# The border of the state space part and attention: last stores in attention's block, first weight and latents split first

## The chip, the cores and the metric

The kernel runs on one core of one Trainium2 chip. The metric is the device time of a run in microseconds (us), lower is better. A core has TensorE (PE, matmuls), VectorE (DVE), ScalarE (ACT), GpSimd (POOL) and SyncE (SP, which in this kernel issues most DMAs). Each has its own instruction stream; they meet through semaphores and, between blocks of the program, at a barrier.

## The reference

One layer of a hybrid diffusion backbone, for 1024 latent tokens and 256 prompt tokens, width 1024, float32. What matters here:

```
h     = rms_norm(x) * (1 + scale) + shift
q_c, kv_c, k_rope, z, xbc, dt_f, dt_b = split(h @ w_in)
ssm   = rms_norm((ssd(xbc, dt_f) + flip(ssd(flip(xbc), dt_b)) + d_skip * x) * silu(z))   # also returns both final states
q     = rms_norm(q_c) @ w_uq          # 4 heads, 128 nope + 64 rope columns
k, v  = [cache_ckv, rms_norm(kv_c)] @ w_ukv
attn  = softmax((q_nope k_nope^T + rope(q_rope) rope(k_rope)^T) * scale) @ v
x     = x + gate * rms_norm(concat(attn, ssm) @ w_out)
x     = x + gate * rms_norm(swiglu(rms_norm(x) * (1 + scale) + shift))
```

Outputs are both token groups, the prompt's normalised latents and rope keys, and the two final states of the state space part.

## The kernel before

**Precision.** A float32 product is made of three matmuls (`split3`, L407): each operand is split into a high part, a copy in the type fp32r that ACT writes, and a low part, raw minus high, that DVE writes. So each operand costs one ACT and one DVE instruction before PE may use it.

**Stages.** `phase_front` is one block: modulation, norm, input projection, and the state space part, chunk by chunk (ten chunks of 128 tokens, c = 0 to 9; NT = 10). `phase_attention` is the next block, `phase_mix_ffn` the last. Blocks are separated by a barrier of all engines, which stands in the trace under L429 (the end of the front's block).

**Chunk loop of the state space part, SP (L642 to L656).** The normalised latents of query (384 rows, three K tiles) and of key and value (256 rows, two K tiles) and the rope keys were written to DRAM scratch before. As each chunk of the state space part is done, its output `zt(c)` (in `chunks_hi`, rows 4 to 7) is stored to DRAM scratch `ssm_mix_scratch` (L656, after ACT's `mix(c)` has counted `mix_ready`), and when that store has landed, the freed columns take the chunk's latents back from scratch (`load_landed`, L417 to L419; the semaphores q_in, kv_in and kr_in count them by block of 512, 512 and 256 tokens). In the last turn, c = 9, SP first waits for `fin_cp` and stores the two final states from `st_in` to the output (L653), then waits for `mix_ready` 10 and stores the last mix. The columns of chunk 9 are loaded at the start of attention's block (L1639, L1640). Weights of head 0 (`wq_raw`, `wk_raw`, `wv_raw`) and the rope table have been loaded earlier (L638, semaphore w_early).

**Start of attention.** The order is written out by hand on every engine:

- ACT: `split(0)`: high parts of query weight (768 columns in each partition), key weight (256), value weight (512). Then the list `landed`, nine entries: query latents by block (3 x 512, 3 x 512, 3 x 256 columns), kv latents by block (2 x 512, 2 x 512, 2 x 256), cache (512), rope keys (1280), cached rope keys (256), each after its load's semaphore. Then the evictions `high` of keys, fold, query and value.
- DVE: the low parts in the same order (`split(0)`, `split_in(0, 3)` for the query latents), then `rotate(0)`, which multiplies the three rope blocks in PSUM by the rope table, then `split_in(3, 9)`, then the low parts of the evicted products.
- PE: `project(0, kind)` for rope columns of the query, keys, fold (adds the rotated halves), query, value. Rope block b waits for b + 1 entries of `in_lo`, key block b for 4, 5, 7; the first product waits for `w_split` 1. A product of 512 columns of tokens is 3 matmuls for each K tile. Five PSUM banks go round (RING): product n waits for the eviction of product n - 5.
- SP: L1639, L1640, clearing of the front's semaphores, and then for h = 1, 2, 3 the weights of head h, after `w_split` h.

After the projections follows the loop over heads and query tiles; ACT splits head 1's weights at query tile 6 of head 0 (L1665).

Of the kernel before, what the change touches and what calls it, by code (L numbers as in the profile page):

```python
# [23 lines left out]
P = 128  # L24
# [10 lines left out]
T = N_LAT + N_PROMPT  # L35
# [386 lines left out]
def phase_front(L):  # L422
# [6 lines left out]
    with ExitStack() as st:  # L429
# [38 lines left out]

        L.rows = in_hi
        L.table = at("rope_table", "hT_lo", 6 * T * 4, [P, T])  # L470
        L.wq_raw = at("wq_raw", "hT_lo", 7 * T * 4, [P, KQ, 256])
# [119 lines left out]
        def _(sp):  # L591
# [50 lines left out]
            for c in range(NT):  # L642
                if c >= 1:
                    sp.wait_ge(mix_stored, 16 * c)
                    load_landed(L, sp, in_hi, c - 1)
                if c - 1 == 5:
                    sp.dma_start(in_hi[:, 3, 0:2 * N_CACHE].rearrange("p (k t) -> p k t", k=2),
                                 L.kv_s.rearrange("a p t -> p a t")[:, :, T:NKEY]).then_inc(L.cache_in, 16)
                    sp.dma_start(in_hi[:, 3, 2 * N_CACHE:3 * N_CACHE], L.kr_s[:, T:NKEY]).then_inc(L.cache_in, 16)
                if c == NT - 1:  # L650
                    sp.wait_ge(fin_cp, 2)
                    for d in range(2):
                        sp.dma_start(L.outs["ssm"][0, 0, d].rearrange("(a h) p n -> (h p) a n", a=4),  # L653
                                     st_in[:, d, :, :]).then_inc(fin_out, 16)
                sp.wait_ge(mix_ready, c + 1)
                sp.dma_start(quads(L.mixS[c]), zt(c)).then_inc(mix_stored, 16)  # L656

# [884 lines left out]
def phase_attention(L):  # L1542
# [3 lines left out]
    with ExitStack() as st:  # L1546
# [22 lines left out]
        part = lambda raw, hi, lo, c, w, sem, n: (raw, hi[:, :, c:c + w], lo[:, :, c:c + w], sem, n)  # L1569
        landed = ([part(rows[:, 4:7, c:c + w], L.qn_hi, L.qn_lo, c, w, L.q_in[b], w // 8) for b, (c, w) in enumerate(BLOCKS)] +  # L1570
                  [part(rows[:, 0:2, c:c + w], L.ckv_hi, L.ckv_lo, c, w, L.kv_in[b], w // 8)
                   for b, (c, w) in enumerate(BLOCKS)] +
                  [part(cache, L.ckv_hi, L.ckv_lo, T, N_CACHE, L.cache_in, 32),
                   (rows[:, 2, :], L.kr_hi[:, 0:T], L.kr_lo[:, 0:T], L.kr_in, 16 * NT),
                   (rows[:, 3, 2 * N_CACHE:3 * N_CACHE], L.kr_hi[:, T:NKEY], L.kr_lo[:, T:NKEY], L.cache_in, 32)])
        rc_ready, rb_ready, in_hi, in_lo = (L.sem("at_" + n) for n in ("rc", "rb", "in_hi", "in_lo"))
# [60 lines left out]
        @block.sync  # L1637
        def _(sp):
            sp.wait_ge(L.mix_stored, 16 * NT)  # L1639
            load_landed(L, sp, rows, NT - 1)  # L1640
            L.clear_old()
            for h in range(1, HEADS):
                sp.wait_ge(w_split, h)
                sp.dma_start(wq_raw[:], L.dram["w_uq"][h]).then_inc(wl, 16)
# [13 lines left out]
        def _(act):  # L1658
            def split(h):
                if h == 0:  # L1660
                    act.wait_ge(L.w_early, 64)
                else:
                    act.wait_ge(wl, 32 * h)
                    act.wait_ge(proj, n_proj(h))
                act.activation(wq_hi[:], wq_raw[:], ACT.Copy).then_inc(w_hi_r, 1)  # L1665
                act.activation(wk_hi[:], wk_raw[:], ACT.Copy).then_inc(w_hi_r, 1)
                if h % 2 == 0:
                    if h >= 2:
                        act.wait_ge(wvl, 16 * (h // 2))
                    act.activation(wv_hi[:], wv_raw[:], ACT.Copy).then_inc(w_hi_r, 1)  # L1670
# [32 lines left out]

            split(0)
            for src, hi, _, sem, n in landed:
# [58 lines left out]
        def _(dve):  # L1764
            c = Chain(dve, dch)

            def split(h):
                dve.wait_ge(w_hi_r, 2 * h + 2 + (h + 1) // 2)
                c.mark(dve.tensor_tensor(wq_lo[:], wq_raw[:], wq_hi[:].bitcast(F32), ALU.subtract))
                c.mark(dve.tensor_tensor(wk_lo[:], wk_raw[:], wk_hi[:].bitcast(F32), ALU.subtract))  # L1770
                if h % 2 == 0:
                    dve.wait_ge(w_hi_r, 2 * h + 3 + h // 2)
                    c.mark(dve.tensor_tensor(wv_lo[:], wv_raw[:], wv_hi[:].bitcast(F32), ALU.subtract))
# [55 lines left out]

            split(0)  # L1830
            split_in(0, 3)
            rotate(0)
            split_in(3, len(landed))
            for kind in order[1:]:
# [53 lines left out]
        def _(pe):  # L1888
            def project(h, kind, only=None):
                for b, n, i in of_kind(h, kind):  # L1890
                    if only not in (None, b):
                        continue
                    if i == 0:
                        pe.wait_ge(w_split, h + 1)
                    if i >= 5:
# [3 lines left out]
                    if h == 0 and kind in ("qrope", "k"):  # L1899
                        pe.wait_ge(in_lo, b + 1 if kind == "qrope" else (4, 5, 7)[b])  # L1900
                    c0, w = stage[kind][b]
# [10 lines left out]
                    else:  # L1912
                        w_hi, w_lo, x_hi, x_lo, kn = ((wk_hi, wk_lo, L.ckv_hi, L.ckv_lo, KKV) if kind == "k" else
                                                      (wq_hi, wq_lo, L.qn_hi, L.qn_lo, KQ))
                        cols = slice(128, 256) if kind == "qrope" else slice(0, 128)
                        for k in range(kn):
                            mm = split3(pe, bank[:, :w], w_hi[:, k, cols], w_lo[:, k, cols], x_hi[:, k, c0:c0 + w],
                                        x_lo[:, k, c0:c0 + w], k == 0, k == kn - 1)
# [1234 lines left out]
```

## Time and profile before

| | |
|---|---|
| median of 3 runs | 1766.49 us (1763.88 to 1767.3) |
| profiled execution | 1768.09 us |
| its span, first to last instruction | 1766.3 us |
| mean granted TensorE clock | 0.982 |
| PE busy | 1677.5 us (95%) |
| DVE busy | 1040.2 us (59%) |
| ACT busy | 725.2 us (41%) |
| first attention matmul | 486.28 us |

The trace holds each instruction with start and duration, what ended an engine's idle time before it, and the clock that PE was granted (1.00 is 2.4 GHz, 0.50 is 1.2 GHz). The border of the change lies at 478 to 502 us of the span. Instructions overlap a little on an engine: the next one starts before the last one's recorded end.

### The profile page before, as it was taken

How to read it: one execution, taken by the hardware profiler on the slowest of the kernel's cores; microseconds unless marked ns; L12 is line 12 of the kernel's file. 1: busy time of each engine (PE TensorE's matmuls, PEld its weight loads, DVE VectorE, ACT ScalarE, POOL GpSimd, SP SyncE). 2: the span in 40 equal slices, each digit the busy share in tenths (PEclk: the TensorE clock that was granted, in tenths of full speed). 3: DMA queues.
4: the chain of work that ended last, by engine and by line, in shares of the span. 5: the costliest groups of instructions: out<-in, count | busy, mean ns of one | idle time of the engine just before them, and what ended most of it. 6: DMA issues, size and time to landing. Idle time of an engine off the chain costs nothing. (4 is left out here: it accounts for less than half of the span.)

```text
span 1766.3 us, 24765 instructions
## 1 busy us (share of the span) xinstructions
PE 1677.5 (95%) x9795; PEld 1500.1 (85%) x9795; DVE 1040.2 (59%) x1581; ACT 725.2 (41%) x1208; POOL 74.6 (4%) x116
## 2 busy tenths in 40 slices
PE   6999899999799999999997999999999998999997
PEld 6787788878678888887887999999999997888885
DVE  5855765328755555574568554555545554467777
ACT  5652323334544444463564333333333333434453
POOL 0100000004300000000000000000000000000000
PEclk9999999999999999999999999999999999999998
DMA  9134242002400000114321222222222225573345
GB/s 370 70 131 139 108 147 75 25 33 54 119 14 19 1 13 1 66 37 156 124 96 37 100 86 84 91 88 93 95 82 85 101 76 194 187 234 97 121 145 196
DMA packets 76290, 176.33 MB, mean 100 GB/s; under 512 B 10352, under 2 KB 26944, under 8 KB 74128
## 3 DMA queue, kind: packets, MB, share of 16 engines
q1 hardware_dynamic: 72080, 169.75, 27.7%
q0 software_dynamic: 4096, 5.01, 0.9%
q8 instruction: 78, 1.28, 0.3%
q14 instruction: 36, 0.29, 0.1%
HBM read 131.02 MB, written 43.70 MB: 99 GB/s over the span
## 5 line engine op out<-in xcount | busy, mean ns | idle before, releaser
L409 PE MATMUL psF<-gv,gu_ring 128*128 128x320 f32 x1232 | 382.5, 310 | 9.2 <-issue 4.6
L410 PE MATMUL psF<-gv,gu_ring 128*128 128x320 f32 x1232 | 382.0, 310 | 0.0
L411 PE MATMUL psF<-gv,gu_ring 128*128 128x320 f32 x1232 | 382.0, 310 | 0.0
L409 PEld LDWEIGHTS psF<-gv,gu_ring 128*128 128x128 f32 x1232 | 232.5, 189 | 10.1 <-issue 9.1
L410 PEld LDWEIGHTS psF<-gv,gu_ring 128*128 128x128 f32 x1232 | 232.4, 189 | 0.0
L411 PEld LDWEIGHTS psF<-gv,gu_ring 128*128 128x128 f32 x1232 | 232.3, 189 | 0.0
L409 PE MATMUL psF<-d_w_ring,d_hid_ring 128*128 128x512 f32 x360 | 141.4, 393 | 6.3 <-DVE d_w_ring L2687 6.3
L410 PE MATMUL psF<-d_w_ring,d_hid_ring 128*128 128x512 f32 x360 | 141.6, 393 | 0.0
L411 PE MATMUL psF<-d_w_ring,d_hid_ring 128*128 128x512 f32 x360 | 141.4, 393 | 0.0
L409 PE MATMUL psP<-hT_hi,win_hi 128*128 128x512 f32 (+1 forms) x336 | 122.9, 366 | 2.3 <-DVE hT_lo L184 1.6
L411 PE MATMUL psP<-hT_hi,win_lo 128*128 128x512 f32 (+1 forms) x336 | 119.7, 356 | 0.0
L410 PE MATMUL psP<-hT_lo,win_hi 128*128 128x512 f32 (+1 forms) x336 | 119.7, 356 | 0.0
L2420 ACT ACTIVATE hraw<-psF 128x320 f32<-128x320 f32 x130 | 56.7, 437 | 152.3 <-PE psF L411 150.8
L2460 ACT ACTIVATE d_hid_ring<-d_hid 128x640 fp32r<-128x640 f32 x72 | 53.3, 740 | 143.2 <-PE psF L411 125.9
L2684 DVE TENSOR_TENSOR d_hid_ring<-d_hid,d_hid_ring 128x640 fp32r<-128x640 f32 x72 | 59.3, 824 | 85.8 <-ACT d_hid_ring L2460 85.5
L409 PEld LDWEIGHTS psF<-d_w_ring,d_hid_ring 128*128 128x128 f32 x360 | 68.5, 190 | 21.6 <-DVE d_hid_ring L2684 7.1
L2633 DVE TENSOR_TENSOR hraw<-hraw,psF 128x320 f32<-128x320 f32 x130 | 62.6, 485 | 41.1 <-ACT hraw L2420 35.0
L1820 DVE TENSOR_TENSOR pt_lo<-psPT,pt_hi 128x512 fp32r<-128x512 f32 (+1 forms) x104 | 58.4, 581 | 40.8 <-ACT pt_hi L1695 40.8
L411 PEld LDWEIGHTS psF<-d_w_ring,d_hid_ring 128*128 128x128 f32 x360 | 68.5, 190 | 14.4
L2416 ACT ACTIVATE gu_ring<-raw_gu 128x512 fp32r<-128x512 f32 x66 | 41.5, 628 | 95.1 <-PE psF L411 95.1
L410 PEld LDWEIGHTS psF<-d_w_ring,d_hid_ring 128*128 128x128 f32 x360 | 68.2, 189 | 14.3
L2616 DVE TENSOR_TENSOR gu_ring<-raw_gu,gu_ring 128x512 fp32r<-128x512 f32 x66 | 45.6, 691 | 49.6 <-ACT gu_ring L2416 49.3
(425 smaller groups left out, 3622.2 us busy)
## 6 DMA issues: line engine op xcount, KB each, us to landing
hid_variants<-hraw SPq DMA_DIRECT2D x77, 320.0 KB, 2.2
d_hid<-hid_variants SPq DMA_DIRECT2D x77, 320.0 KB, 3.0
m_wring<-in_w_mod SPq DMA_DIRECT2D x16, 1024.0 KB, 5.5
d_b<-in_w_down SPq DMA_DIRECT2D x44, 256.0 KB, 3.8
win_raw<-in_w_in SPq DMA_DIRECT2D x18, 512.0 KB, 5.7
w_mod_staged<-in_w_mod SPq DMA_DIRECT2D x16, 512.0 KB, 11.8
raw_gu<-in_w_gate SPq DMA_DIRECT2D x11, 512.0 KB, 3.9
raw_gu<-in_w_up SPq DMA_DIRECT2D x11, 512.0 KB, 4.8
```

The costliest lines, as they stand in the source:

```text
L409: pe.matmul(out, w_hi, x_hi, start=first, stop=False, skip_group_check=onto)
L410: pe.matmul(out, w_hi, x_lo, start=False, stop=False, skip_group_check=onto)
L411: return pe.matmul(out, w_lo, x_hi, start=False, stop=last, skip_group_check=onto)
L1820: dve.tensor_tensor(pt_lo[:, g[0]:g[-1] + 1, r:r + P], psPT[:, (g0 + i) % 2, 0:len(g), :], pt_hi[:, g[0]:g[-1] + 1, r:r + P].bitcast(F32), ...
L2416: act.activation(wv[:, q % R, 0, :], block_of(r, n), ACT.Copy).then_inc(wv_hi, 1)
L2420: act.activation(dst[:, chunk(c)], psA(c), ACT.Copy).then_inc(copied, 1)
L2460: act.activation(ring_h(e, 0), hr[:, e % 3, :], ACT.Copy).then_inc(h_hi, 1)
L2616: dve.tensor_tensor(wv[:, q % R, 1, :], block_of(r, n), wv[:, q % R, 0, :].bitcast(F32), ALU.subtract).then_inc(wv_lo, 1)
L2633: dve.tensor_tensor(dst[:, chunk(c)], src[:, chunk(c)], bank(c), ALU.add).then_inc(added, 1)
L2684: dve.tensor_tensor(ring_h(e, 1), hr[:, e % 3, :], ring_h(e, 0).bitcast(F32), ALU.subtract).then_inc(h_lo, 1)
```

## The change

SP leaves the front's block after the load of chunk 8's latents. The store of the last mix and the two stores of the final states are issued first thing in attention's block, the mix store ahead of the others, and without waits: the barrier orders them. `split(0)` is gone from ACT and DVE; the three weights of head 0 are entries of `landed`, which now has 14: query weight, the three K tiles of the first query block one by one, second query block, key weight, first kv block, third query block, second and third kv block, cache, rope keys, cached rope keys, value weight. DVE makes the first eight before `rotate(0)` (N_ROPE). PE's rope blocks wait for 1, 5 and 8 entries, block 0 besides for its K tile k's entry (k + 2) ahead of that tile's matmuls; key blocks wait for 8, 9 and 11, the value products for all 14. The weights of head 1 are loaded once all 14 are split; `w_split` and `w_hi_r` count from head 1.

```diff
--- before.py
+++ after.py
@@ -467,6 +467,7 @@
 
 
         L.rows = in_hi
+        L.last_mixed, L.st_out = in_hi[:, 4:8, (NT - 1) * P:NT * P], st_in
         L.table = at("rope_table", "hT_lo", 6 * T * 4, [P, T])
         L.wq_raw = at("wq_raw", "hT_lo", 7 * T * 4, [P, KQ, 256])
         L.wk_raw = at("wk_raw", "hT_lo", 7 * T * 4 + KQ * 1024, [P, KKV, P])
@@ -647,13 +648,9 @@
                     sp.dma_start(in_hi[:, 3, 0:2 * N_CACHE].rearrange("p (k t) -> p k t", k=2),
                                  L.kv_s.rearrange("a p t -> p a t")[:, :, T:NKEY]).then_inc(L.cache_in, 16)
                     sp.dma_start(in_hi[:, 3, 2 * N_CACHE:3 * N_CACHE], L.kr_s[:, T:NKEY]).then_inc(L.cache_in, 16)
-                if c == NT - 1:
-                    sp.wait_ge(fin_cp, 2)
-                    for d in range(2):
-                        sp.dma_start(L.outs["ssm"][0, 0, d].rearrange("(a h) p n -> (h p) a n", a=4),
-                                     st_in[:, d, :, :]).then_inc(fin_out, 16)
-                sp.wait_ge(mix_ready, c + 1)
-                sp.dma_start(quads(L.mixS[c]), zt(c)).then_inc(mix_stored, 16)
+                if c < NT - 1:
+                    sp.wait_ge(mix_ready, c + 1)
+                    sp.dma_start(quads(L.mixS[c]), zt(c)).then_inc(mix_stored, 16)
 
         @block.gpsimd
         def _(pool):
@@ -1567,12 +1564,18 @@
         rows = L.rows
         cache = rows[:, 3, 0:2 * N_CACHE].rearrange("p (k t) -> p k t", k=2)
         part = lambda raw, hi, lo, c, w, sem, n: (raw, hi[:, :, c:c + w], lo[:, :, c:c + w], sem, n)
-        landed = ([part(rows[:, 4:7, c:c + w], L.qn_hi, L.qn_lo, c, w, L.q_in[b], w // 8) for b, (c, w) in enumerate(BLOCKS)] +
-                  [part(rows[:, 0:2, c:c + w], L.ckv_hi, L.ckv_lo, c, w, L.kv_in[b], w // 8)
-                   for b, (c, w) in enumerate(BLOCKS)] +
-                  [part(cache, L.ckv_hi, L.ckv_lo, T, N_CACHE, L.cache_in, 32),
+        q0, q1, q2 = (part(rows[:, 4:7, c:c + w], L.qn_hi, L.qn_lo, c, w, L.q_in[b], w // 8)
+                      for b, (c, w) in enumerate(BLOCKS))
+        kv0, kv1, kv2 = (part(rows[:, 0:2, c:c + w], L.ckv_hi, L.ckv_lo, c, w, L.kv_in[b], w // 8)
+                         for b, (c, w) in enumerate(BLOCKS))
+        first_w = [(raw[:], hi[:], lo[:], L.w_early, 64)
+                   for raw, hi, lo in ((wq_raw, wq_hi, wq_lo), (wk_raw, wk_hi, wk_lo), (wv_raw, wv_hi, wv_lo))]
+        landed = ([first_w[0]] + [tuple(x[:, k, :] for x in q0[:3]) + q0[3:] for k in range(KQ)] +
+                  [q1, first_w[1], kv0, q2, kv1, kv2, part(cache, L.ckv_hi, L.ckv_lo, T, N_CACHE, L.cache_in, 32),
                    (rows[:, 2, :], L.kr_hi[:, 0:T], L.kr_lo[:, 0:T], L.kr_in, 16 * NT),
-                   (rows[:, 3, 2 * N_CACHE:3 * N_CACHE], L.kr_hi[:, T:NKEY], L.kr_lo[:, T:NKEY], L.cache_in, 32)])
+                   (rows[:, 3, 2 * N_CACHE:3 * N_CACHE], L.kr_hi[:, T:NKEY], L.kr_lo[:, T:NKEY], L.cache_in, 32),
+                   first_w[2]])
+        N_ROPE, ROPE_AT, K_AT = 8, (1, 5, 8), (8, 9, 11)
         rc_ready, rb_ready, in_hi, in_lo = (L.sem("at_" + n) for n in ("rc", "rb", "in_hi", "in_lo"))
         units = [(h, t) for h in range(HEADS) for t in range(NT)]
         key_tiles = lambda t: list(range(NT_LAT, NT)) if t >= NT_LAT else list(range(NT_LAT)) + [NT, NT + 1]
@@ -1636,11 +1639,18 @@
 
         @block.sync
         def _(sp):
+            sp.dma_start(L.mixS[NT - 1].rearrange("p (a n) -> p a n", n=P), L.last_mixed).then_inc(L.mix_stored, 16)
+            for d in range(2):
+                sp.dma_start(L.outs["ssm"][0, 0, d].rearrange("(a h) p n -> (h p) a n", a=4),
+                             L.st_out[:, d, :, :]).then_inc(L.fin_out, 16)
             sp.wait_ge(L.mix_stored, 16 * NT)
             load_landed(L, sp, rows, NT - 1)
             L.clear_old()
             for h in range(1, HEADS):
-                sp.wait_ge(w_split, h)
+                if h == 1:
+                    sp.wait_ge(in_lo, len(landed))
+                else:
+                    sp.wait_ge(w_split, h - 1)
                 sp.dma_start(wq_raw[:], L.dram["w_uq"][h]).then_inc(wl, 16)
                 sp.dma_start(wk_raw[:], L.dram["w_uk"][h]).then_inc(wl, 16)
                 if h % 2 == 0:
@@ -1657,16 +1667,12 @@
         @block.scalar
         def _(act):
             def split(h):
-                if h == 0:
-                    act.wait_ge(L.w_early, 64)
-                else:
-                    act.wait_ge(wl, 32 * h)
-                    act.wait_ge(proj, n_proj(h))
+                act.wait_ge(wl, 32 * h)
+                act.wait_ge(proj, n_proj(h))
                 act.activation(wq_hi[:], wq_raw[:], ACT.Copy).then_inc(w_hi_r, 1)
                 act.activation(wk_hi[:], wk_raw[:], ACT.Copy).then_inc(w_hi_r, 1)
                 if h % 2 == 0:
-                    if h >= 2:
-                        act.wait_ge(wvl, 16 * (h // 2))
+                    act.wait_ge(wvl, 16 * (h // 2))
                     act.activation(wv_hi[:], wv_raw[:], ACT.Copy).then_inc(w_hi_r, 1)
 
             def high(h, kind):
@@ -1701,7 +1707,6 @@
                     act.wait_ge(o_read, pair)
                 act.activation(rb[:], psO[:, 2 * P:4 * P], ACT.Copy).then_inc(rb_ready, 1)
 
-            split(0)
             for src, hi, _, sem, n in landed:
                 act.wait_ge(sem, n)
                 act.activation(hi, src, ACT.Copy).then_inc(in_hi, 1)
@@ -1765,11 +1770,11 @@
             c = Chain(dve, dch)
 
             def split(h):
-                dve.wait_ge(w_hi_r, 2 * h + 2 + (h + 1) // 2)
+                dve.wait_ge(w_hi_r, 2 * h - 1 + (h + 1) // 2)
                 c.mark(dve.tensor_tensor(wq_lo[:], wq_raw[:], wq_hi[:].bitcast(F32), ALU.subtract))
                 c.mark(dve.tensor_tensor(wk_lo[:], wk_raw[:], wk_hi[:].bitcast(F32), ALU.subtract))
                 if h % 2 == 0:
-                    dve.wait_ge(w_hi_r, 2 * h + 3 + h // 2)
+                    dve.wait_ge(w_hi_r, 2 * h + h // 2)
                     c.mark(dve.tensor_tensor(wv_lo[:], wv_raw[:], wv_hi[:].bitcast(F32), ALU.subtract))
                 c.wait()
                 dve.sem_inc(w_split, 1)
@@ -1827,10 +1832,9 @@
                     dve.wait_ge(in_hi, i + 1)
                     dve.tensor_tensor(lo, src, hi.bitcast(F32), ALU.subtract).then_inc(in_lo, 1)
 
-            split(0)
-            split_in(0, 3)
+            split_in(0, N_ROPE)
             rotate(0)
-            split_in(3, len(landed))
+            split_in(N_ROPE, len(landed))
             for kind in order[1:]:
                 low(0, kind)
             dve.wait_ge(L.fin_out, 32)
@@ -1890,14 +1894,16 @@
                 for b, n, i in of_kind(h, kind):
                     if only not in (None, b):
                         continue
-                    if i == 0:
-                        pe.wait_ge(w_split, h + 1)
+                    if i == 0 and h >= 1:
+                        pe.wait_ge(w_split, h)
                     if i >= 5:
                         pe.wait_ge(drained, n - 4)
                     elif h >= 1:
                         pe.wait_ge(e_ready, h * NT - (0 if i == 4 else 1 if i == 3 else 2))
                     if h == 0 and kind in ("qrope", "k"):
-                        pe.wait_ge(in_lo, b + 1 if kind == "qrope" else (4, 5, 7)[b])
+                        pe.wait_ge(in_lo, (ROPE_AT if kind == "qrope" else K_AT)[b])
+                    elif h == 0 and kind == "v":
+                        pe.wait_ge(in_lo, len(landed))
                     c0, w = stage[kind][b]
                     bank = psS[:, RING[i % 5], :]
                     if kind == "fold":
@@ -1914,6 +1920,8 @@
                                                       (wq_hi, wq_lo, L.qn_hi, L.qn_lo, KQ))
                         cols = slice(128, 256) if kind == "qrope" else slice(0, 128)
                         for k in range(kn):
+                            if (h, kind, b) == (0, "qrope", 0):
+                                pe.wait_ge(in_lo, k + 2)
                             mm = split3(pe, bank[:, :w], w_hi[:, k, cols], w_lo[:, k, cols], x_hi[:, k, c0:c0 + w],
                                         x_lo[:, k, c0:c0 + w], k == 0, k == kn - 1)
                     mm.then_inc(proj, 1)
```

## Rows read from the trace of the kernel before

**Rows 1.** Page, part 1: busy us, share of span, instructions
```profile
PE 1677.5 (95%) x9795; PEld 1500.1 (85%) x9795; DVE 1040.2 (59%) x1581; ACT 725.2 (41%) x1208; POOL 74.6 (4%) x116
```

**Rows 2.** PE's waits over the span: us in total, times, longest us
```profile
PE psScore L409 <- DVE qn_lo L1828: 8.1, 1, 8.1
...
PE psF L409 <- issue: 4.6, 1, 4.6
```

**Rows 3.** Timeline of PE: start, duration, instruction, idle before and releaser
```profile
486.28 0.77 PE L409 MATMUL psScore<-qn_hi,wq_hi 128*128 128x512 f32 x1 [8.12 <-DVE qn_lo L1828]
...
491.31 0.40 PE L409 MATMUL psScore<-qn_hi,wq_hi 128*128 128x512 f32 x1
...
491.54 0.40 PE L410 MATMUL psScore<-qn_lo,wq_hi 128*128 128x512 f32 x1
...
495.56 0.50 PE L409 MATMUL psScore<-ckv_hi,wk_hi 128*128 128x512 f32 x1 [1.65 <-DVE ckv_lo L1828]
...
501.75 0.58 PE L409 MATMUL psScore<-qn_hi,wq_hi 128*128 128x512 f32 x1
```

**Rows 4.** Timeline of SP at the border: start, duration, instruction
```profile
474.78 0.52 SPq L656 DMA_DIRECT2D ssm_mix_scratch<-chunks_hi  x1
477.36 0.37 SPq L417 DMA_DIRECT2D chunks_hi<-q_scratch  x1
...
478.31 0.47 SPq L419 DMA_DIRECT2D chunks_hi<-kr_scratch  x1
...
479.84 0.64 SPq L656 DMA_DIRECT2D ssm_mix_scratch<-chunks_hi  x1
483.31 0.37 SPq L417 DMA_DIRECT2D chunks_hi<-q_scratch  x1
```

**Rows 5.** L429, end of the front's block: drains in ns, start in us
```profile
L429 POOLq DRAIN  x1: 2888/2888/2888, 476.0 to 476.0; - x1
...
L429 ACTq DRAIN  x1: 626/626/626, 478.2 to 478.2; - x1
L429 SPq DRAIN  x1: 368/368/368, 480.5 to 480.5; - x1
```

**Rows 6.** Timeline of ACT: start, duration of all x, idle before
```profile
481.15 0.84 ACT L1665 ACTIVATE wq_hi<-wq_raw 128x768 fp32r<-128x768 f32 x1 [2.35 <-PEq L429]
...
482.20 0.61 ACT L1670 ACTIVATE wv_hi<-wv_raw 128x512 fp32r<-128x512 f32 x1
482.72 2.84 ACT L1707 ACTIVATE qn_hi<-chunks_hi 128x1536 fp32r<-128x1536 f32 x2
485.95 0.84 ACT L1707 ACTIVATE qn_hi<-chunks_hi 128x768 fp32r<-128x768 f32 x1 [0.39 <-DMA chunks_hi<-q_scratch]
486.70 1.99 ACT L1707 ACTIVATE ckv_hi<-chunks_hi 128x1024 fp32r<-128x1024 f32 x2
```

**Rows 7.** Windows: stretch, length, busy of PE, PEld, DVE, ACT, POOL, PEclk, DMA, GB/s
```profile
392.20:398.80 6.60, 6.60 (x18) 4.20 (x19) 0.86 (x1) 2.15 (x2) 2.51 (x3) 0.50 0.03 3
...
490.00:491.00 1.00, 1.00 (x4) 0.81 (x3) 0.51 (x1) 1.00 (x2) 0.00 (x0) 0.50 0.03 8
...
935.00:938.00 3.00, 2.78 (x10) 2.81 (x11) 3.00 (x4) 1.27 (x1) 0.00 (x0) 0.50 0.00 0
```

**Rows 8.** Timeline of DVE
```profile
482.33 0.96 DVE L1769 TENSOR_TENSOR wq_lo<-wq_raw,wq_hi 128x768 fp32r<-128x768 f32 x1 [4.52 <-ACT wk_hi L1666]
...
484.37 4.29 DVE L1828 TENSOR_TENSOR qn_lo<-chunks_hi,qn_hi 128x1536 fp32r<-128x1536 f32 x3
490.49 0.69 DVE L1782 TENSOR_TENSOR q_prod<-psScore,rope_table 128x512 f32<-128x512 f32 x1 [1.83 <-PE psScore L411]
...
494.30 3.55 DVE L1828 TENSOR_TENSOR ckv_lo<-chunks_hi,ckv_hi 128x1024 fp32r<-128x1024 f32 x4
...
499.50 1.88 DVE L1794 TENSOR_TENSOR kn_lo<-psScore,kn_hi 128x512 fp32r<-128x512 f32 x3
```

**Rows 9.** ACT's split of head 1's query weight: ns, first and last start
```profile
L1665 ACT ACTIVATE wq_hi<-wq_raw x1: 833/833/833, 549.0 to 549.0; 128x768 fp32r<-128x768 f32 x1
```

## The prediction

> **What bounds the kernel now.** I read the page first: TensorE (PE) is busy 95% of the span [rows 1], so only time in which it waits or runs at its lower clock can be given back. The list of PE's waits comes next: its longest single wait, 8.1 us, stands before the first matmul of attention, for `qn_lo` [rows 2]. The timeline around it gives the pieces. PE's last work of the state space part ends at 486.28 - 8.12 = 478.16 [rows 3]. Before the barrier between the two blocks (L429) ScalarE (ACT) has drained at 478.2 + 0.63 = 478.83 and GpSimd (POOL) at 476.0 + 2.89 = 478.89, but SyncE (SP) drains only at 480.54 to 480.91, behind its stores [rows 4, 5]. ACT then starts at 481.15 and splits the weights of query, key and value and the first latents before PE may begin [rows 6]. PE runs its first matmuls at half clock (1.2 instead of 2.4 GHz): the stretch 490 to 491 has 0.50 [rows 7], and matmuls of 512 columns then start 0.43 us apart (twice 0.23, the distance between 491.31 and 491.54 [rows 3]). It waits once more, 1.65 us, for `ckv_lo`, and begins the keys at 495.56 and the first query block at 501.75 [rows 3]. VectorE (DVE) has by then been through six splits, 494.30 to 499.50 [rows 8].
>
> **The change, part by part.** I follow the new order to 501.75's counterpart, since from there on the code and the order of work are the old ones.
>
> *Barrier.* SP's last work before it is now the issue of L419, which ends at 478.31 + 0.47 = 478.78; the two state stores (479.84 - 478.78 = 1.06 us with gaps) and the last mix store (0.64) are taken out [rows 4]. From the end of L656 (480.48) to ACT's start (481.15) were 0.67 us [rows 4, 6]. With SP free at 478.78, and POOL's drain over (478.89) before SP's own would be (0.37 from 478.8, so 479.2 [rows 5]), ACT starts at about 479.4: 1.7 us gained. Bounds: 0, if something unseen holds the barrier, and 1.8, where ACT or POOL would end it.
>
> *Stores and last loads.* They are now issued after the barrier, the mix store first: 479.4. Such a store took 474.78 to 477.36 = 2.58 us until the waiting load left, and 3.47 behind the state stores [rows 4]; now it is ahead of them: 2.6, so L417 leaves at 482.0 and, like before (483.31 to 485.95 [rows 4, 6]), is there 2.6 later: 484.6, or 485.5 at the upper bound of both. The state stores have one reader of their end, a wait of DVE (L1836) that stands behind all first projections. The clearing of semaphores behind L417 to L419 has no waiter.
>
> *ACT.* From starts in [rows 6]: 512 columns cost 0.52, 1536 (2.84 - 1.47) = 1.37, so 0.21 for each 256 more; 1024 (1.99 - 1.04) = 0.95; the two weights of 768 and 256 columns 481.15 to 482.20 = 1.05 together, 0.74 and 0.31 by the slope. New order: query weight 479.4 to 480.24 (its own duration 0.84), the three K tiles of the first latents from 480.14, 480.66, 481.18, second latents 481.70 to 483.16, key weight 483.07, first kv block 483.38, and at 484.33 the last latents, which then wait for their load. Even from 485.5 they are done at 486.35.
>
> *DVE.* From [rows 8]: 512 columns cost (1.88 - 0.68)/2 = 0.60, 1536 (4.29 - 0.96)/2 = 1.67; by the slope 0.27 for each 256, 256 cost 0.33, 768 0.87, 1024 1.13. `wq_lo` starts 0.03 behind its high part: 480.27. K tile 0 is split from 481.14 to 481.83. PE began 0.15 after its input before (484.37 + 1.76 = 486.13 to 486.28 [rows 8, 3]): now 481.98 instead of 486.28, 4.30 earlier. The split into three K tiles costs DVE 3 x 0.60 - 1.67 = 0.13, hidden: tiles 1 and 2 are there by 483.03, and PE needs 1.28 us for each at half clock. Then the second latents at 483.2 (ACT), key weight 484.87, kv block 485.20, last latents 486.33, done at 487.29.
>
> *PE.* Rope columns of the query: 18 matmuls at 0.23 and 9 at half that, 5.18 us at full clock, plus half of the slow stretch S. Before, S was 491.0 - 486.28 = 4.7. After another idle time, of 4.6 us [rows 2], the clock was low from 935 to 938 (0.50), with PE busy for most of it [rows 7]; the idle time here is now 3.8. I take S = 3.4, between 2.8 (935 to 938) and 4.7; bounds 0 and 6.6, the last because PE ran 6.6 us on end, wholly busy, at 0.50 in 392.2 to 398.8 [rows 7]. Blocks 0 and 1 end at 481.98 + 4.14 + 1.7 = 487.82, later than the last latents (487.29), so no wait; block 2 ends at 488.86. The keys begin at once, since their first block is split already: 495.56 becomes 488.86, and 1.80 us between the last rope issue (486.28 + 5.18 + 2.35 = 493.8) and 495.56 go.
>
> *What is late next.* DVE now turns the three rope products before it splits the second kv block. The last starts 0.2 after PE's end, 489.05; kv block 1 runs 489.39 to 490.61; PE ends its first key block at 488.86 + 1.38 = 490.24 and waits 0.4. The next input (the cache) is there at 491.8, before 492.0. From there DVE has the old five splits and the value weight: 5.20 - 1.13 + 0.60 = 4.67, so the first `kn_lo` starts at 494.06 and the second ends at 495.35. Before, keys to query block took 501.75 - 495.56 = 6.19 [rows 3]; now 488.86 + 6.19 + 0.4 = 495.45, just not held by `kn_lo`.
>
> *Value weight and next weights.* The value weight moves behind all latents; its 0.60 is in the 4.67. Value products need it 5 us and more after 495. SP loads head 1's weights once everything is split, at about 494.8, some microseconds later than before; they are wanted at 549.0 [rows 9]. That is 50 us of cover; only without it would the delay, under 10 us, count.
>
> *Sum.* 501.75 - 495.45 = 6.3 us: 4.30 (barrier 1.75, order 2.55) + 0.65 (shorter slow stretch) + 1.80 - 0.4, within rounding. It runs on to the end because PE's order behind it is unchanged and relative to its own ends. The profiled execution took 1768.09 (span 1766.3 and 1.8 around it), so it would be 1761.8; the median of the runs shown, 1766.49, is 1.6 lower: 1760.2.
>
> **A rule of the skill.** The trace gives one execution, whose slow stretch began and ended where it did once. The Trainium skill, "TensorE: Matmul & The Clock Gate", section "What's actually happening", says that the gate's timing runs free of the kernel, and that one kernel showed 6, 11 or 14 slow matmuls. An estimate by that page: 6 to 14 at 0.43 us are S = 2.6 to 6.0 and a gain of 6.7 to 5.0. No run here shows the spread; the forecast stays by the rows.
>
> **Rivals.**
> - *The barrier does not come earlier* (the change does not do what it says): for it, GpSimd's drain of 2.89 us ends at 478.89, so something slow sits there too; against, SP's drain is the last of all by 2 us [rows 5]. Gain 6.3 - 1.7 = 4.6, time 1761.9; with S = 6.6 as well, 3.0 and 1763.5.
> - *The gain is given back later*: an engine other than PE sets the pace in attention's loop or at a later border, and PE only waits longer there. For it, 5% of the span are idle; against, by the code nothing behind the first projections waits for the border itself, and the weight loads have their 50 us. Gain 0 to 3, time about 1765.
> - *Slower: the clock stays low.* PE starts early on thin supply, and the half clock granted at 481 is not given back through rope, keys, fold and query. Each microsecond of S costs 0.5; from S = 3.4 + 2 x 6.3 = 16 us the kernel is slower; at S = 22, through the query columns, 6.3 - 9.3 = -3.0, time 1769.5. For it, 6.6 us of busy PE at 0.50 [rows 7]; against, before it came back after 4.7 us of unbroken work [rows 3, 7], and the new work is unbroken from 481.98 on.
>
> **From this the numbers.** The forecast (gain 4.7 to 6.8) 0.70; barrier unchanged 0.12; given back 0.14; slower 0.04. Low end: S = 0 gives 6.8, 1759.7; other slow stretches of the kernel fall differently in each execution, one like 935 to 938 is worth about 1.5, and the runs shown lie 3.4 apart: 1757.4. High end: gain 3.0 and little more, 1763.8. What this kernel's measurement can tell from no change is about 0.2%, 3.5 us, so faster means under 1763.0: all of the forecast, most of the second, a little of the third: 0.82. Within: 0.14. Slower: 0.04.
>
> **What would show it.** After: ACT starts attention 0.6 to 0.7 us after L419's issue ends; PE idle 3.8 us before its first rope matmul, released by K tile 0 of `qn_lo`; no idle between rope and keys, about 0.4 us before the second key block; the first query block starts 6.3 us earlier relative to the state space part; head 1's `wq_hi` and the waits of later stages as before. It is wrong if PE's wait moves into a K tile or the last latents, if the slow stretch has over 7 us of PE's work, or if the 6 us are there at 500 and not at the end.

## The result, and the profile after

The changed kernel took 1756.24 us, the median of 4 runs (1753.9 to 1759.24), beside 1766.66 for the kernel before (4 runs); ratio 0.9945, 95% interval 0.9926 to 0.9963. The forecast was 1760.2 in a range of 1757.4 to 1763.8: the sign was right, the time lies 1.2 us below the range. Later, 17 more runs of the changed kernel and 91 of the one before on three chips gave, with all earlier ones, means of 1756.8 (21 runs, standard error 0.5) and 1764.0 (95 runs, 0.2): 7.2 us, standard error 0.6. The first eight runs showed 10.

The profiled execution took 1759.24 us, span 1757.4. PE's waits have lost their longest single one: of the 8.1 us before the rope stage [rows 2], 3.9 are left, in two waits.

```profile
PE psScore L409 <- DVE qn_lo L1833: 3.9, 2, 3.6
```

The drains of L429 in the changed kernel (ns, start in us) answer to [rows 5]: SP is over at 476.8 + 0.12 = 476.9, just behind ACT's (476.75) and level with POOL's (476.9).

```profile
L429 POOLq DRAIN  x1: 2888/2888/2888, 474.0 to 474.0; - x1
...
L429 ACTq DRAIN  x1: 626/626/626, 476.1 to 476.1; - x1
L429 SPq DRAIN  x1: 122/122/122, 476.8 to 476.8; - x1
```

SP's timeline answers to [rows 4]: the mix store leaves after the barrier and waits 2.67 us (477.11 to 479.78), not 3.47.

```profile
476.23 0.47 SPq L419 DMA_DIRECT2D chunks_hi<-kr_scratch  x1
477.11 0.52 SPq L1642 DMA_DIRECT2D ssm_mix_scratch<-chunks_hi  x1
...
477.68 1.22 SPq L1644 DMA_DIRECT2D out_ssm<-st_in  x2
479.78 0.37 SPq L417 DMA_DIRECT2D chunks_hi<-q_scratch  x1
```

ACT's timeline [rows 6]: its last work of the state space part starts at 476.12, attention 1.00 us later; the last query latents are awaited for 1.88 us.

```profile
476.12 0.60 ACT L918 ACTIVATE chunks_hi<-psP 128x512 f32<-128x512 f32 x1 [0.81 <-PE psP L1416]
477.12 0.84 ACT L1712 ACTIVATE wq_hi<-wq_raw 128x768 fp32r<-128x768 f32 x1 [0.40 <-PEq L429]
...
484.02 0.85 ACT L1712 ACTIVATE qn_hi<-chunks_hi 128x768 fp32r<-128x768 f32 x1 [1.88 <-DMA chunks_hi<-q_scratch]
```

DVE's timeline [rows 8]: K tiles one after the other, then a wait for the last latents, then the second kv block behind the rope products.

```profile
478.87 1.89 DVE L1833 TENSOR_TENSOR qn_lo<-chunks_hi,qn_hi 128x512 fp32r<-128x512 f32 x3
...
484.90 0.96 DVE L1833 TENSOR_TENSOR qn_lo<-chunks_hi,qn_hi 128x768 fp32r<-128x768 f32 x1 [0.74 <-ACT qn_hi L1712]
...
487.64 2.42 DVE L1833 TENSOR_TENSOR ckv_lo<-chunks_hi,ckv_hi 128x1024 fp32r<-128x1024 f32 x3
...
492.32 1.88 DVE L1799 TENSOR_TENSOR kn_lo<-psScore,kn_hi 128x512 fp32r<-128x512 f32 x3
```

PE's timeline [rows 3]: first rope matmul, third rope block, first and second key block, first query block.

```profile
479.70 0.47 PE L409 MATMUL psScore<-qn_hi,wq_hi 128*128 128x512 f32 x1 [3.61 <-DVE qn_lo L1833]
...
485.92 0.39 PE L409 MATMUL psScore<-qn_hi,wq_hi 128*128 128x256 f32 x1 [0.27 <-DVE qn_lo L1833]
...
487.10 0.40 PE L409 MATMUL psScore<-ckv_hi,wk_hi 128*128 128x512 f32 x1
...
488.91 0.50 PE L409 MATMUL psScore<-ckv_hi,wk_hi 128*128 128x512 f32 x1 [0.27 <-DVE ckv_lo L1833]
...
493.77 0.58 PE L409 MATMUL psScore<-qn_hi,wq_hi 128*128 128x512 f32 x1
```

The windows [rows 7]: low clock only in a part of 480 to 484 (mean 0.57, so 3.4 us at 0.50), 1.00 on both sides.

```profile
476.00:480.00 4.00, 0.39 (x2) 0.30 (x2) 2.00 (x3) 3.48 (x6) 0.00 (x0) 1.00 0.77 219
480.00:484.00 4.00, 4.00 (x12) 3.13 (x11) 3.82 (x5) 2.15 (x3) 0.00 (x0) 0.57 0.68 178
484.00:488.00 4.00, 3.73 (x21) 2.96 (x20) 3.02 (x6) 3.98 (x6) 0.00 (x0) 1.00 0.01 2
```

Head 1's weights are still wanted 50 us later [rows 9].

```profile
L1672 ACT ACTIVATE wq_hi<-wq_raw x2: 836/836/836, 541.0 to 612.0; 128x768 fp32r<-128x768 f32 x2
```

To compare traces whose state space part ends at different times, I measure the border from ACT's last mix copy (L921, after L918) to PE's first query block. Before, that copy starts at

```profile
478.20 0.60 ACT L921 ACTIVATE chunks_hi<-psP 128x512 f32<-128x512 f32 x1 [0.81 <-PE psP L1419]
```

so the border took 501.75 - 478.20 = 23.55 us, and after it takes 493.77 - 476.12 = 17.65: 5.90 us less. Of the 8.9 us between the two spans, 2.08 lie ahead of the copy, where the code is the same, and 0.9 behind the query block.

### The profile page after: what moved, and what is told of

Same layout as the page of the kernel before. It is cut to its first block and busy times, and to the rows that moved or that the text cites. A ratio compares the mean times of both kernels' runs of the same rounds, so it can differ in the third digit from the quotient of the medians.

```text
span 1757.4 us, 24774 instructions
## 1 busy us (share of the span) xinstructions
PE 1673.5 (95%) x9795; PEld 1497.4 (85%) x9795; DVE 1040.1 (59%) x1583; ACT 724.5 (41%) x1210; POOL 74.7 (4%) x116
## 5 line engine op out<-in xcount | busy, mean ns | idle before, releaser
L1701 ACT ACTIVATE pt_hi<-psPT 128x512 fp32r<-128x512 f32 (+1 forms) x104 | 52.1, 514 | 55.5 <-PE psPT L1967 54.3
```

The lines of the kernel that those rows point to most:

```text
L1701: act.activation(pt_hi[:, g[0]:g[-1] + 1, r:r + P], psPT[:, (g0 + i) % 2, 0:len(g), :], ACT.Copy).then_inc(pth_ready, 1)
```

## The experiments

Each kernel was run beside the kernel before, in three groups of four that each shared a chip and its runs of before: `again_after`, `again_before`, `stores_only`, `order_only` (27 runs of before, mean 1764.2); `after_2`, `loads_first`, `whole_block`, `warm` (25, 1763.2); `before_warm`, `warm_2`, `warm_k`, `state_first` (28, 1764.4). Gains are differences of means from the runs of before on the same chip (for the changed kernel, all runs against all), with one standard error. "Border" is the measure above, in the one trace of each. S is PE's time at half clock within the border, from its first rope matmul on.

| kernel | runs | mean us | gain on before | border | S |
|---|---|---|---|---|---|
| before | 95 | 1764.0 | | 23.55, 23.22 | 4.7, 3.4 |
| changed | 21 | 1756.8 | 7.2 +- 0.6 | 17.65, 18.25, 17.08 | 3.4, 5.9, 3.4 |
| `stores_only` | 12 | 1762.7 | 1.6 +- 0.9 | 20.97 | 3.4 |
| `order_only` | 10 | 1758.0 | 6.2 +- 1.1 | 20.39 | 5.7 |
| `loads_first` | 12 | 1757.2 | 6.0 +- 0.9 | 18.25 | 5.8 |
| `whole_block` | 8 | 1756.8 | 6.4 +- 0.7 | 19.69 | 4.7 |
| `warm` | 5 | 1755.4 | 7.8 +- 0.8 | 16.81 | 0 |
| `warm_2` (the same) | 11 | 1759.1 | 5.3 +- 0.8 | 17.98 | 0 |
| `warm_k` | 9 | 1759.5 | 4.9 +- 0.9 | 18.00 | 0 |
| `state_first` | 9 | 1759.3 | 5.1 +- 1.1 | 18.25 | 5.9 |
| `before_warm` | 12 | 1762.6 | 1.9 +- 0.9 | 22.05 | 0 |

**The two kernels again.** `again_after`, `after_2` and `again_before` are the kernels unaltered.

> The changed kernel unaltered, timed again in more rounds. In the traces the change is worth 5.9 us at the border itself (ScalarE's last mix copy to the first query block: 23.55 us before, 17.65 after); 2.1 of the 8.9 us between the two profiled spans lie ahead of the border, where the code is the same. Theory A (the mechanism of the prediction at nearly its size, the rest is how the slow clock stretches fell in eight runs): 5 to 8 us faster than before, ratio 0.9955 to 0.997. Theory B (something real outside the border gives 4 us more): 10 us faster, ratio 0.9945 again.

> The kernel before against itself, in as many rounds: what two identical programs show as a difference. Theory A: medians up to 2 us apart, single runs 3 to 5 us apart, and each run's time goes with its mean granted clock. Theory B: medians within 0.5 us.

> The changed kernel again, as the base for the three beside it and for a larger sample. Theory A (border alone, 5.0 to 5.9 us in two pairs of traces, the rest sampling of the clock): the mean of all its runs moves from 7.7 us faster towards 6. Theory B (2 us more from outside the border): it stays at 7.5 or more.

Measured: `again_after` ratio 0.9950 (0.9936 to 0.9963), `again_before` 0.9998 (0.9989 to 1.0006, its medians 1.3 us apart, as theory A said), `after_2` 0.9967 (0.9956 to 0.9978). Single runs of before lie between 1758.5 and 1769.0. The gain moved from 10 to 7.7 +- 1.5 and 6.1 +- 0.8 with larger samples, as theory A said; the two weighted by their errors make 6.4 +- 0.7. The pooled 7.2 +- 0.6 holds the first eight runs, which raised the question. It lies above the 5.7 of the borders' means (23.39 less 17.66) by 2.5 standard errors of the whole alone, the 6.4 by one; the borders' means, of two and three traces, have an error of their own. Behind the query block, no difference is shown: 1264.5 and 1262.0 us to the end of the span before, 1263.7, 1261.8 and 1261.1 after.

**The two halves apart.** `stores_only` is the kernel before with the SyncE part of the diff (both hunks of SP and the names `last_mixed`, `st_out`); `order_only` is the changed kernel with SP's old lines back (and the three stores at the start of attention's block gone):

```diff
-                if c < NT - 1:
-                    sp.wait_ge(mix_ready, c + 1)
-                    sp.dma_start(quads(L.mixS[c]), zt(c)).then_inc(mix_stored, 16)
+                if c == NT - 1:
+                    ...
+                sp.wait_ge(mix_ready, c + 1)
+                sp.dma_start(quads(L.mixS[c]), zt(c)).then_inc(mix_stored, 16)
```

> The kernel before with the SyncE part of the change alone: last mix store and state stores in attention's block, weights and latents split in the old order. Theory A: the barrier ends 1.95 us earlier, and the whole is 1.9 to 2.2 us faster (ratio 0.9989). Rival C (the last latents, now loaded behind the state stores, take 4.2 instead of 2.6 us and hold ScalarE and VectorE): gain 0.5 or less.

> The changed kernel with SyncE's old order at the border: the stores before the barrier again, the new order of splits kept. Theory A: barrier as before, first rope matmul 2.55 us after where it would be by the barrier instead of 5.13, no late key inputs: 4.0 to 4.5 us faster (ratio 0.9975). Theory B: with the stores' part about 2, this shows 8.

`stores_only` in its trace: copy at 479.13, attention at 480.13, the same 1.00 us as after; the old 1.65 us before the keys is there.

```profile
480.13 0.84 ACT L1666 ACTIVATE wq_hi<-wq_raw 128x768 fp32r<-128x768 f32 x1 [0.40 <-PEq L429]
```
```profile
493.88 0.50 PE L409 MATMUL psScore<-ckv_hi,wk_hi 128*128 128x512 f32 x1 [1.65 <-DVE ckv_lo L1829]
```

`order_only`: copy at 473.14 and attention 3.23 us after it, as before, but PE starts 2.58 us behind ACT instead of 5.13, exactly as in the changed kernel (479.70 - 477.12).

```profile
476.37 0.84 ACT L1711 ACTIVATE wq_hi<-wq_raw 128x768 fp32r<-128x768 f32 x1 [2.63 <-PEq L429]
```
```profile
478.95 0.76 PE L409 MATMUL psScore<-qn_hi,wq_hi 128*128 128x512 f32 x1 [5.85 <-DVE qn_lo L1832]
```

`order_only` gained 6.2 +- 1.1, more than the 4.0 to 4.5 expected but by under two standard errors; its border is 3.0 us shorter with S = 5.7, which would be 4.1 with the 3.4 that I reckoned with. Theory B wanted 8.

So the order of splits is the larger half, and within the error the gains add up to the whole: 1.6 + 6.2 = 7.8 +- 1.4 beside 7.2 +- 0.6. Rival C of `stores_only` (a gain of 0.5 or less, from latents that take 4.2 us) is not excluded by the whole time. In its trace the border is 2.4 us shorter, but the latents took 2.96 us there, so what late ones cost in the old order is not shown.

**The late latents.** `loads_first` moves the state stores behind the three loads; `state_first` puts them ahead of the mix store.

`loads_first`, shortened:

```diff
             sp.dma_start(L.mixS[NT - 1].rearrange(...), L.last_mixed).then_inc(L.mix_stored, 16)
-            for d in range(2):
-                sp.dma_start(L.outs["ssm"]...).then_inc(L.fin_out, 16)
             sp.wait_ge(L.mix_stored, 16 * NT)
             load_landed(L, sp, rows, NT - 1)
+            for d in range(2):
+                sp.dma_start(L.outs["ssm"]...).then_inc(L.fin_out, 16)
```

> The changed kernel with the two state stores issued behind the loads of the last chunk (mix store, wait, three loads, then the state stores). In the changed kernel the last query latents took 4.2 us to land and PE waited 0.4 us for them before rope block 2. If they land late because the state stores are ahead of them: here 2.6 us, ScalarE's wait of 1.88 us shrinks to about 0.3, PE's 0.4 goes, the border is 0.4 to 0.8 us shorter; the whole kernel 0 to 1 us faster than the changed one. Rival (the landing is slow for another reason, the length of the wait is the same): border unchanged within 0.1.

> The changed kernel with the two state stores ahead of the last mix store in attention's block, the old order of the three. If the mix store is landed later because of them: SP's wait ends 1.1 us (issue) + 3.5 instead of 2.7 after the barrier, so the last query latents' load leaves 1.9 us later, is there 2.6 to 4.2 later, and rope block 2 waits 0.5 to 2 us: border 0.5 to 2 us longer than in the changed kernel, total 0.5 to 2 us more. Rival (slack of VectorE's chain hides it): border and total unchanged.

From L417's issue to ACT's use of the latents (485.84 less 483.27, and so on): with the state stores between mix store and load, 4.24 and 4.56 and 2.84 in the changed kernel, 3.1, 4.6, 4.65, 2.9 and 3.0 in `warm`, `warm_2`, `warm_k`, `whole_block` and `stores_only`; with them ahead of the mix store 2.57 in `state_first` and 2.6 in the kernel before; behind the loads 3.45. So a load right behind them is late (over 4 us) in four traces of eight and in none of the others. That the two stores are the cause is not shown: `loads_first` did not get the 2.6 that I expected, although the DMA engines were idle (share 0.00) in the half microsecond behind the load's issue. `state_first`:

```profile
483.27 0.37 SPq L417 DMA_DIRECT2D chunks_hi<-q_scratch  x1
```
```profile
485.84 0.85 ACT L1712 ACTIVATE qn_hi<-chunks_hi 128x768 fp32r<-128x768 f32 x1 [1.88 <-DMA chunks_hi<-q_scratch]
```

What the late ones have in common can be seen in the windows. In all eight traces the 16 DMA engines are fully busy (share about 1.0) from before the load's issue until 1 us after it, and the share has fallen under 0.35 by 3.0 us. In the late four a share of 0.05 to 0.08, about one engine of 16, then goes on for another microsecond or more; in the other four it is 0.00 by 3.5 us. The changed kernel's first trace (load issued at 479.78, latents used at 484.02), and below it `after_2` (478.70, used at 481.54):

```profile
483.00:484.00 1.00, 1.00 (x4) 0.77 (x4) 1.00 (x2) 0.00 (x0) 0.00 (x0) 0.63 0.07 17
```
```profile
482.00:483.00 1.00, 1.00 (x5) 0.84 (x4) 1.00 (x1) 1.00 (x2) 0.00 (x0) 0.85 0.01 2
```

For the border it hardly counts: with S near 5.9 it took 18.25 in `again_after`, `loads_first` and `state_first` alike, although the latents were there 8.2, 7.0 and 7.9 us after the copy. Only with the short S of 3.4 did the late load show, 17.65 against 17.08. I expected `state_first` to lose 0.5 to 2 us; at the border its rival, that the slack hides it, held. The whole time cannot tell: 5.1 +- 1.1 gained beside 7.2 +- 0.6, but the other two variants of the changed kernel on that chip have 5.3 and 4.9 as well.

**The K tiles.** `whole_block` has the first query latents as one entry:

```diff
-        landed = ([first_w[0]] + [tuple(x[:, k, :] for x in q0[:3]) + q0[3:] for k in range(KQ)] +
+        landed = ([first_w[0], q0] +
-        N_ROPE, ROPE_AT, K_AT = 8, (1, 5, 8), (8, 9, 11)
+        N_ROPE, ROPE_AT, K_AT = 6, (2, 3, 6), (6, 7, 9)
-                            if (h, kind, b) == (0, "qrope", 0):
-                                pe.wait_ge(in_lo, k + 2)
```

> The changed kernel without the K tile split: the first 512 tokens of query latents are one entry again (14 entries become 12), the order otherwise kept. PE can start when the whole first block is split: ScalarE 0.74 + 1.47, VectorE 1.76 + 0.15 behind it, so 4.1 us after ScalarE's start instead of 2.6; PE would then not be caught again by the last latents. Theory A: first rope matmul 1.5 us later, block 2 no longer waits, so border 1.0 to 1.5 us longer than the changed one, the kernel 1 to 1.5 us slower than it. Rival (VectorE sets the end of the rope stage anyway): under 0.3 us.

```profile
475.14 0.84 ACT L1712 ACTIVATE wq_hi<-wq_raw 128x768 fp32r<-128x768 f32 x1 [0.88 <-PEq L429]
```
```profile
479.20 0.79 PE L409 MATMUL psScore<-qn_hi,wq_hi 128*128 128x512 f32 x1 [5.58 <-DVE qn_lo L1833]
```

PE starts 4.06 us behind ACT instead of 2.58, so the tiles are worth 1.5 us at the start, as expected. The border was 19.69: 0.5 of it is a later barrier and 0.65 the longer S (4.7 against 3.4), which leaves 18.5 beside 17.08 and 17.65. The whole time shows no loss (6.4 +- 0.7 gained), and cannot tell 1.5 us from none.

**The clock.** `warm` adds three matmuls that nobody reads to the changed kernel, `before_warm` five of them to the kernel before; `warm_k` is `warm` with the second query latents split by K tiles too.

```diff
+            for n in range(3):
+                pe.matmul(psPT[:, 0, :, :], L.ident, L.const[:, 0:4 * P].rearrange("p (a n) -> p a n", n=P), start=True, stop=True)
             for kind in order:
                 project(0, kind)
```

> The changed kernel with three float32 matmuls of 128 by 512 constants into a PSUM bank that is free then, at the start of attention on PE: work that nobody reads, 2.6 us, in PE's idle time at the border. If PE's slow stretch comes from the idle time: the granted clock stays at 1.00 through the border, rope blocks run at 0.23 us a matmul, and PE then waits for K tiles, the second latents and the last latents instead; at most 1.7 us gained, by the input times 0.5 to 1.2 us. Rival (the clock falls all the same): nothing gained, or 0.2 lost where the last of the three ends behind the first input.

> The kernel before, with five float32 matmuls of 128 by 512 constants that nobody reads at the start of attention on PE (4.4 us in its 5.1 us between barrier and first rope matmul). It prices the slow clock at the border in the old order. If the slow stretch costs half of PE's work in it (3.4 to 4.7 us in three traces): 1.5 to 2.4 us faster than before, ratio 0.9990, and no low clock between 478 and 495 in the trace. Rival (2.9 us of idle time ahead of the barrier lower the clock all the same): low clock under the dummy matmuls, gain 0 to 1.

> The changed kernel with three dummy matmuls again, for a sample. In its first five runs it was 1.4 us (two standard errors of 0.9) below the mean of 21 runs of the changed kernel; in its trace the clock stayed at 1.00, and the border took 16.81 us against 17.08 to 18.26. If the clock is the cause: again 0.8 to 1.6 us below the changed kernel, ratio to before 0.9955 to 0.996. Rival (sampling): within 0.5 us of the changed kernel's 1756.8.

> As the one before, and the second 512 tokens of query latents split by K tiles too. With the clock at 1.00, PE waited 0.72 us for these latents as a whole. By K tiles the first is there 1.1 us earlier, VectorE pays 0.13 us more: PE's 0.7 us wait goes, but keys wait for VectorE's chain (0.3 us before now), so 0 to 0.4 us at the border, not to be told apart in the whole. Rival (the rope stage is PE's to end): 0.7 us.

In `warm` the clock stayed at 1.00, the three took 2.81 us, and PE then waited 0.72 us for the second latents as a whole:

```profile
478.00:480.00 2.00, 2.00 (x7) 1.00 (x6) 2.00 (x4) 2.00 (x4) 0.00 (x0) 1.00 1.06 288
```
```profile
476.77 2.81 PE L1997 MATMUL psPT<-const 128*128 128x512 f32 x6 [1.06 <-PEq L429]
...
482.37 0.50 PE L409 MATMUL psScore<-qn_hi,wq_hi 128*128 128x512 f32 x1 [0.72 <-DVE qn_lo L1833]
```

In the trace of `warm_2`, the same kernel, the clock fell under them, they took 4.51 us, and the first rope matmul came 1.4 us late:

```profile
478.00:480.00 2.00, 2.00 (x4) 0.77 (x3) 2.00 (x4) 2.00 (x3) 0.00 (x0) 0.50 1.06 289
```
```profile
476.49 4.51 PE L1997 MATMUL psPT<-const 128*128 128x512 f32 x6 [1.06 <-PEq L429]
```

The lead of 1.4 us that `warm` had over the changed kernel in five runs did not come back in eleven; my expectation for `warm_2` failed, and its mean of 1759.1 is not within 0.5 of 1756.8 either, as the rival had it. Over both, the gain on before is 6.5 +- 0.6.

`warm_k` removed the 0.72 us wait, its clock stayed at 1.00, and yet its border is 18.00, 1.2 us longer than that of `warm`. PE waited for the last latents instead, whose load was one of the late ones (4.65 us against 3.11 in `warm`), so the split itself is not tested by this trace:

```profile
486.00 0.39 PE L409 MATMUL psScore<-qn_hi,wq_hi 128*128 128x256 f32 x1 [2.21 <-DVE qn_lo L1833]
```

So at full clock a late load sets the end of the rope stage (in `warm_2` PE waits 0.48 us for it). `before_warm` had the low clock under its dummies, which is the sign of the rival and not of my theory, and its first rope matmul comes 0.4 us later behind ACT (5.51 us, not 5.13). It was 1.3 us shorter at the border and gained 1.9 +- 0.9 in all, a size that does not tell the two apart. No version beat the changed kernel by more than the errors.

## Why the prediction was right or wrong

- **Barrier.** The mechanism was right, the size a little over its bound: 1.7 with 1.8 at most was said, and from copy to attention it is 1.00 instead of 2.95 us, so 1.95 (2.2 against `again_before`, 3.20). SP's drain after loads alone took 0.12, not the 0.37 that I carried over, and ACT starts 0.42 us after L419's issue ends, not 0.6 to 0.7; ACT, POOL and SP are now done within 0.2 us of each other.
- **Order of splits.** Right to the digit: 2.58 us from ACT's start to PE's was in the working (479.4 to 481.98), and is in every trace with K tiles and without dummies.
- **Slow stretch.** S = 3.4 was the value in two of three traces, 5.9 in the third, within the bounds; each microsecond of S costs about 0.5, as 17.08 and 18.25 show (1.17 for 2.43). The page's statement that the gate runs free of the kernel (the Trainium skill, "TensorE: Matmul & The Clock Gate", "What's actually happening") agrees with these traces: one program, two sizes of S.
- **Stores and last loads.** The mix store was right (2.6 said, 2.67). The load behind the state stores was mis-sized: 2.6 with 3.5 as the bound, 4.2 to 4.65 in half of the traces. In the changed kernel it costs up to 0.6 us at the border: in the first trace PE waits 0.27 us for these latents, where the working had no wait.
- **What is late next.** Right: 0.27 us before the second key block (0.4 said), keys straight behind the rope stage, `kn_lo` not in the way. The border by the working was 495.45 - 478.20 = 17.25; the three traces have 17.08, 17.65 and 18.25. The 0.2 us to 17.08 are the barrier's; 17.65 has the late load besides and 18.25 the longer S.
- **Later stages.** Nothing is seen to be given back behind the query block, so the rival with a gain of 0 to 3 is out, and so is the slower one; the traces rule out the unmoved barrier.

**The step that failed** is the one that turned the gain into a time, the last sentence of *Sum* (1766.49 less 6.3 is 1760.2) and the low end of the range. I took the median of three runs, 1766.49, as the level of before. The mean of 95 runs is 1764.0 with single runs over 10 us, and a median as high as 1766.49 comes up in one of twenty draws of three out of the 91 later runs. From that level the working gives 1764.0 - 6.3 = 1757.7, 0.9 above the 1756.8 of 21 runs. So of the 4.0 us between 1760.2 and 1756.24, 2.5 are the level of before, 0.9 the gain and 0.6 the four runs of the changed kernel, whose median lies below the mean of the 21. Whether the first runs of before were high by chance or by something in that session stays open; the changed kernel's runs beside them were not (1756.4 on the mean). The range went down to 1757.4 because I allowed 2.3 us below the largest gain for slow stretches elsewhere, and took the spread from three runs (3.4 us).

The gain itself, 6.3, is not shown to be wrong: it lies 1.5 standard errors below the pooled 7.2 +- 0.6, and beside the 6.4 +- 0.7 of the two later comparisons it is met. Nor is a part of the gain seen in the granted clock elsewhere in the kernel. Its mean over the span is 0.9843 in 80 runs of before and 0.9858 in the 21 of the changed kernel, so (1 - clock) x span is 27.7 us and 24.9: 2.8 +- 0.8 less, or 5.7 us less time at half clock. At the border alone the low clock lasted 10.2 us in both traces of before, and 3.4, 6.8 and 3.4 after, partly over an idle PE: 5.7 less on the mean, the same amount. As far as five traces tell, the border holds all of it, and what the low clock costs there is in the 5.7 us between the borders' lengths already. Whether anything real lies between those 5.7 us and the 7.2 of all runs stays open. Over all kernels' runs the time rises by 0.43 us for each microsecond of (1 - clock) x span, with 1.7 us of scatter left: the clock explains a part of the spread of single runs.

## What to carry to other kernels

Work out the border between two stages as a chain of its own, instruction by instruction: which engine arrives last at the barrier, what the first consumer waits for, and what stands in each queue ahead of it; here that gave the start of PE behind ACT's to a hundredth of a microsecond. Make the first operands the ones PE needs first and in the pieces in which it uses them, and hand over stores that nobody reads soon behind the barrier. And when the gain sought is 0.4%, the level of before is a term like any other: three runs give it to 2 or 3 us only, so the range needs that width on both sides before any mechanism is added.

## What the runs showed of the hardware that was not expected

- SP's drain at L429 took 0.37 us in the four traces where its last issue was a store, and 0.12 us in the ten where it was a load, each begun within 0.1 us of the end of that issue.
- A load of 192 KB issued about 1 us behind two stores of 256 KB each from the same queue took 2.84, 4.24 and 4.56 us in three traces of one program, and about 2.6 us where the stores were further ahead. In the late cases a share of 0.05 to 0.08 of the DMA engines, about one of 16, went on for a microsecond after the rest was done. That the stores cause it is not shown: behind idle engines `loads_first` took 3.45.
- Filling an idle gap of PE with idle matmuls is no sure way to keep its clock: with 1.06 us of idle time left ahead of them it stayed at 1.00 in two traces (`warm`, `warm_k`) and fell in one (`warm_2`), where the dummies themselves ran slow and delayed the real work by 1.4 us.
